# Joining the band stage to the recurrence: barrier taken out, gates made in the band, two z tiles moved, decay sums in rounded halves

## The reference, cut to what matters

```python
xn = _rmsnorm(h, norm_mix_w[l])
proj = xn @ w_in[l]
q_a, k_a, v_a, qkv_g, z_g, a_g, b_g = jnp.split(proj, SPLIT_POINTS, axis=-1)
attn = _windowed_gqa(q_a, k_a, v_a, band_bias, in_window, attn_sink[l])     # 8 heads, +-128 keys

# the mixer beside it
qkv = jax.nn.silu(_centred_conv(qkv, conv_w)).astype(f32)                   # 5 taps
q, k, v = jnp.split(qkv, 3, axis=-1)                                        # q, k then l2-normed
g = -jnp.exp(a_log.astype(f32)) * jax.nn.softplus(a + dt_bias.astype(f32))
beta = jax.nn.sigmoid(b)
o_fwd = _chunk_gated_delta_rule(q, k, v, g[:, :, 0], beta[:, :, 0])
o_bwd = flip(_chunk_gated_delta_rule(flip(q), flip(k), flip(v), flip(g[:, :, 1]), flip(beta[:, :, 1])))
o = _rmsnorm(o_fwd + o_bwd, norm_w) * jax.nn.silu(z)
h = h + jnp.concatenate([attn, gdn], axis=-1) @ w_out[l]
```

## Time and profile before

| | |
|---|---|
| median of 3 runs | 2480.06 us (2477.2 to 2482.18) |
| the profiled execution | 2485.23 us |
| its span in the trace | 2483.5 us |
| PE busy in it | 2390.8 us |
| band stage with a PE that is never idle | 108.4 to 372.9 us |
| from there to the first product of `front(0)` | 372.9 to 401.26 us |
| to `levels(0)` | 454.48 us |

### The profile page before, as it was taken

How to read it: one execution, slowest core, us unless ns; L and a number is a source line. 1 busy time by engine, 2 the same in 40 slices (tenths; PEclk the granted TensorE clock), 3 DMA queues, 4 the chain that set the end, 5 groups by cost and what they waited for, 6 DMA issues and landing times.

```text
span 2483.5 us, 32754 instructions
## 1 busy us (share of the span) xinstructions
PE 2390.8 (96%) x12918; PEld 2032.2 (82%) x12918; DVE 1071.9 (43%) x1652; ACT 803.6 (32%) x1353; POOL 750.2 (30%) x527
## 2 busy tenths in 40 slices
PE   7999996899899999999999999999999999999999
PEld 5888885899877888887888878988888788888887
DVE  5266624455445644352222253123333253556633
ACT  4144555222412422232121321144444112565101
POOL 2222112343322577762222223221111241111250
PEclk9999998899998999999999989999999999999999
DMA  6722212223343234344232205523441346343441
GB/s 207 224 58 62 68 53 70 63 57 75 118 144 112 86 118 170 119 138 159 93 99 71 68 17 210 156 75 86 113 119 51 132 161 158 106 109 140 135 160 68
DMA packets 252091, 274.95 MB, mean 111 GB/s; under 512 B 43730, under 2 KB 204280, under 8 KB 249897
## 3 DMA queue, kind: packets, MB, share of 16 engines
q1 hardware_dynamic: 229928, 217.31, 29.4%
q10 hardware_dynamic: 22016, 55.61, 6.1%
HBM read 188.91 MB, written 86.08 MB: 111 GB/s over the span
## 4 chain that ended last, share of the span: by engine, by line
PE 91%; DVE 3%; DMA 2%; ACT 1%; issue 1%; POOL 1%; POOLq 0%; SPq 0%; ACTq 0%; DVEq 0%
PE PS L302 19%; PE PS L1948 13%; PE PS L283 10%; PE PS L1929 10%; PE PS L2256 4%; PE PS L3059 4%; PE PS L2915 3%; PE PS L2211 3%; PE PS L2469 2%; PE PS L410 2%; PE PS L1961 2%; PE PS L1334 2%; PE PS L1328 2%; PE PS L706 1%; PE PS L2458 1%; PE PS L2754 1%
## 5 line engine op out<-in xcount | busy, mean ns | idle before, releaser
L250 POOL CAST Wh<-Wraw 128x1024 fp32r<-128x1024 f32 x72 | 75.8, 1053 | 882.2 <-PE PS L302 575.7
L1948 PE MATMUL PS<-op_h,fw_h 128*128 128x512 f32 x512 | 200.3, 391 | 3.6 <-POOL fw_l L1843 3.6
L1948 PE MATMUL PS<-op_l,fw_h 128*128 128x512 f32 x512 | 200.1, 391 | 0.0
L1948 PE MATMUL PS<-op_h,fw_l 128*128 128x512 f32 x512 | 200.1, 391 | 0.0
L252 POOL TENSOR_TENSOR Wl<-Wraw,Wh 128x1024 fp32r<-128x1024 f32 x72 | 176.3, 2448 | 10.4
L1843 POOL TENSOR_TENSOR fw_l<-draw,fw_h 128x512 fp32r<-128x512 f32 x64 | 84.7, 1325 | 257.8 <-ACT fw_h L1984 257.8
L1843 POOL TENSOR_TENSOR fw_l<-fraw,fw_h 128x512 fp32r<-128x512 f32 x92 | 126.3, 1386 | 95.5 <-ACT fw_h L1984 95.4
L1929 PE MATMUL PS<-op_h,fw_h 128*128 128x512 f32 x392 | 152.5, 389 | 0.0
L1929 PE MATMUL PS<-op_l,fw_h 128*128 128x512 f32 x392 | 152.5, 389 | 0.0
L1929 PE MATMUL PS<-op_h,fw_l 128*128 128x512 f32 x392 | 152.5, 389 | 0.0
L302 PE MATMUL PS<-XAh,Wh 128*128 128x512 f32 x328 | 134.3, 410 | 2.1 <-POOL Wl L252 2.1
(11 more groups left out here) (472 smaller groups left out, 5929.3 us busy)
## 6 DMA issues: line engine op xcount, KB each, us to landing
Wraw<-in_w_in SPq DMA_DIRECT2D x66, 512.0 KB, 4.2
fraw<-in_w_ffn_in SPq DMA_DIRECT2D x16, 1024.0 KB, 5.3
f_scr<-blocks SPq DMA_DIRECT2D x16, 1024.0 KB, 4.3
draw<-in_w_ffn_out SPq DMA_DIRECT2D x32, 512.0 KB, 4.1
stage<-f_scr SPq DMA_DIRECT2D x24, 512.0 KB, 4.6
x_scr<-hT SPq DMA_DIRECT2D x2, 4096.0 KB, 13.5
Wraw<-in_w_out SPq DMA_DIRECT2D x16, 512.0 KB, 4.0
gate_scr<-gbuf ACTq DMA_DIRECT2D x16, 512.0 KB, 2.7
```

The source lines that it names most:

```text
L250: pool.tensor_copy(Wh[:, slot], Wraw[:, slot])
L1948: mm = pe.matmul(dense_bank(n)[:, 512 * b:512 * b + 512], w_, x_, start=(k == 0 and m == 0), stop=(k == KT - 1 and m == 2))
```

## The change

Four things are done at once.

1. "phase1" joins `JOINED`: no barrier between band and recurrence. Buffers and PSUM banks are placed anew and waits are added in its stead.
2. The tile with a and b becomes the first of the tiles in the band. Its 8 transposes stand in unit 6, `act_softplus` and `dve_gates` in units 7 to 9, `pe_gates` behind the last unit. The zeros for `wy_scr` and `wt_scr` are written at the start of phase 1, from a buffer of zeros. The transposes of the recurrence's first chunk come ahead of the attention's last `turn_out`.
3. The band keeps 15 of the 17 tiles. The last two of z (96 products) are made in `pe_prep`: 8 products behind each of six chunks' transposes, the remaining 48 in a row ahead of `front(1)`. ACT takes them out and makes their silu behind `decays(1)`.
4. `gate` is divided into `gate_h` and `gate_l` (fp32r). `decay_rhs` makes two operands for each unit, and PE makes each decay sum as two fp32r products in place of one f32 product. ACT writes the exponentials into `qkT` in place of a buffer of their own.

Besides, `WY` and `WT` are loaded in eight pieces (the pieces for e = 0 first), the load for p = 0 waits until the last late product is made, and `load_att(sp, 0)` waits for the last update of the state (`d_s`, 7) where it waited for `d_o2` and `d_acc` of an earlier step.

```diff
-        BAND_FILL = list(range(N_CONV, N_AB + 1))
+        TILES = list(range(N_AB, N_OUT1))
+        LATE_Z = 2
+        BAND_FILL = TILES[:-LATE_Z]
+        AB_TURN = 6
...
             sp.dma_start(x_scr, hT[:]).then_inc(spill, 16)
+            sp.wait_ge(zeros_made, 1)
+            for scr in (wy_scr, wt_scr):
+                sp.dma_start(bass.AP(scr.tensor, 0, [[4 * GH * MAT // P, P], [4 * (P + 1), 4], [1, 4 * (P + 1)]]),
+                             zeros[:].unsqueeze(1).to_broadcast([P, 4, 4 * (P + 1)])).then_inc(setup_dma, 16)
...
             values(UW - 1)
-            pe.wait_ge(ab_sb, 1)
-            pe.wait_ge(w_pt, UW)
-            for t in range(NT):
-                mm = pe.transpose(PS[:, 4, t * 16:(t + 1) * 16], cpad[0][0:16, 2 + t * P:2 + (t + 1) * P], ident[0:16, 0:16])
-            mm.then_inc(ab_t, 1)
+            pe_gates(pe)
+            pe_turn_chunk(pe, 0)
             turn_out(NT - 1)
...
+            act_gates(act)
+            act_squares(act, 0)
             copy_out(NT - 1)
+            act_root(act, 0)
             store_out(NT - 1)
-            for i in range(2):
-                act.wait_ge(z_out[i], 32)
-            act.wait_ge(att_out, 32 * NT)
...
+        def late_z(pe):
+
+            for h in range(2 * LATE_Z):
+                f, b = Z0F + h // 2, h % 2
+                n = N_AB + f
+                if h == 0:
+                    pe.wait_ge(w_out, NT)
+                    pe.wait_ge(w_hi, NT)
+                elif b:
+                    pe.wait_ge(half_free, f + 1)
+                elif h == 2:
+                    pe.wait_ge(ps_free, n)
+                if b == 0:
+                    pe.wait_ge(w_ready, n + 1)
+                for c, (k, hi, lo) in enumerate(model):
+                    for w, x, m in ((Wh, hi, 0), (Wh, lo, 1), (Wl, hi, 2)):
+                        mm = pe.matmul(PS[:, Z_BANKS[h], :], w[:, n % 2, k], x[:, b * 512:(b + 1) * 512],
+                                       start=(c == 0 and m == 0), stop=(c == KT - 1 and m == 2))
...
-                if p >= 2:
+                if p == 0:
+                    sp.wait_ge(mm_done, N_OUT1)
+                elif p >= 2:
...
+                for e in range(2):
+                    for x, scr in ((WY_all, wy_scr), (WT_all, wt_scr)):
+                        for d in range(2):
+                            u = 2 * d + e
+                            sp.dma_start(x[p % 2][:, u], scr[u * GH:(u + 1) * GH, 0:P, :].rearrange("m p c -> p m c")
+                                         ).then_inc(wu_in[e], 16)
...
             for d in range(2):
-                sp.wait_ge(d_o2[d], NT - 2)
-                sp.wait_ge(d_acc[d], NT - 2)
+                sp.wait_ge(d_s[d], NT - 1)
+                sp.wait_ge(d_kd[d], NT)
+            sp.wait_ge(att_out, 32 * NT)
             load_att(sp, 0)
...
-                    pe.matmul(bank(d, 2 + e), tri[:, 2 + d], gl[e][d].rearrange("p h c -> p (h c)"), start=True, stop=True
-                              ).then_inc(d_dt[d], 1)
+                    for x in (gl_h[p // 2], gl_l[p // 2]):
+                        mm = pe.matmul(bank(d, 2 + e), strict[d][:], x[e][d].rearrange("p h c -> p (h c)"),
+                                       start=(x is gl_h[p // 2]), stop=(x is gl_l[p // 2]))
+                    mm.then_inc(d_dt[d], 1)
...
-            pe_prep(pe, 0)
+            fill = late_z(pe)
+            pe_prep(pe, 0, fill, (0, 8, 8, 8, 0))
             front(0)
             for d in range(2):
                 pe.wait_ge(d_kq[d], 2)
-            pe_prep(pe, 4)
+            pe_prep(pe, 4, fill, (8, 8, 8, 0, 0))
+            for _ in fill:
+                pass
             front(1)
...
+                if p == 0:
+                    pe.wait_ge(zeros_made, 2)
                 steps(p)
...
-        JOINED = ("phase5", "phase7", "phase9", "phase12", "phase14")
+        JOINED = ("phase1", "phase5", "phase7", "phase9", "phase12", "phase14")
```

More of the change, by code:

```diff
@@ L1015, in pe_prep @@
+        def pe_prep(pe, first, fill, quota):
+            for i in range(first, first + 5):
+                if i < first + 4 and i:
+                    pe_turn_chunk(pe, i)
+                for _ in range(quota[i - first]):
+                    next(fill)
                 if i > first:
@@ L1028, in act_softplus @@
             act.activation(gt[:, 1], gt[:, 0], ACT.Abs)
[L1029 removed]
+            act.activation(small[:, 0, 8:16], rows[:, 0:8], ACT.Exp)
             act.activation(beta[:], abT[:, :, 8:16], ACT.Exp, scale=-1.0).then_inc(beta_exp, 1)
@@ L1209, in sp_phase4 @@
                 sp.wait_ge(d_kd[d], NT)
+            for i in range(2):
+                sp.wait_ge(z_out[i], 32)
             sp.dma_start(zT[:], z_scr.rearrange("j p t -> p j t")).then_inc(z_back, 16)
@@ L1259, in pool_phase4 @@
             pool.wait_ge(blk_solved, 1)
+            qk_masked(0)
+            for d in range(2):
+                pool.wait_ge(d_dt[d], 4)
             k_gated(0)
-            qk_masked(0)
+            pool.wait_ge(mm_done, N_OUT1)
             k_decayed(0)
@@ L1265, in pool_phase4 @@
                     qk_masked(p + 1)
+                if p == 0:
+                    for i in range(LATE_Z):
+                        pool.wait_ge(z_out[i], 32)
+                    for d in range(2):
+                        pool.memset(St[d][:], 0.0)
+                    pool.memset(oacc[:], 0.0).then_inc(zeros_made, 1)
                 if p + 2 < NP2:
```

273 lines of the change are left out of this document (170 added, 103 removed).

## The result

The changed kernel takes 2464.8 us (median of 5, 2460.71 to 2469.49) where the kernel before takes 2480.06: a ratio of 0.9931, 95% interval 0.992 to 0.9943. It is faster by 15.3 us at the medians, 17 by the ratio. The forecast was 35 us with a range of 2435 to 2462, so the time lies outside it, on the slow side.

The account below looks back on a forecast made before the run. PE, busy 96% of the span, was taken as the bound. Terms -20.2 - 9.1 - 8.3 - 2.2 + 3.4 + 1 = -35.4 us; from the 2480.06 median this gave 2445 us, 8-in-10 range 2435 to 2462.

Parts of the forecast that it names:

- The band: Band before the recurrence: 96 products leave, saving 21.9 us; a and b add 0.7, hiccups 1; sum -20.2 us.
- the start: Kernel's start: 2 MB of zeros go ahead of `load_q(2)`, costing 0 to 5 us; +1 taken.
- B: Time mark from which the forecast counts: the end of the band's last values, 372.90 us in the trace before.
- the rival that the band is not PE's: In the band PE waits for DVE's maxima: total 2457, or 2467 if all 21.9 us are lost; chance 0.14.
- To `front(0)`: From the band's end to `front(0)`: starts at B+22 instead of B+28.4, 6.4 us less, with 24 moved products inside.
- `front(0)`: Recurrence's first front: 11.0 us at full clock, where it took 14.72 at clock 0.82; ends at B+33.0.
- Solving and the 48 products: After `front(0)`: blocks solved at B+57.0 without gain; 48 products (11.0) and a bank exchange (0.5) end at B+62.3.
- `levels(0)` at B+72.5: Start of the first pair's levels, where loads and `front(1)` meet: 9.1 us earlier than B+81.6.
- The first level at 8.85 us: First level of `levels(0)`: with PE hardly pausing before it, 8.85 us instead of 17.16, so -8.3 us.
- `front(2)` and `front(3)`: Later fronts of the recurrence: each saves 1.1 us, together -2.2.
- The end of the recurrence: Attention, `zT` and w_out loads queue behind the last state update; ACT's second rounding ends later: +3.4 us.
- The rival of the low clock: PE's clock stays low in the recurrence's first stretch: 8.3 us and up to 5 more, total 2458; chance 0.16.

Follow-up runs that it names:

- e8: Changed kernel, but DVE takes the attention's low part out of its bank between the first chunk's sum of squares and its root; ratio to the kernel before 0.9909.
- e6: Changed kernel, but ACT's two waits for stores stand ahead of the first late z half's eviction, not ahead of the exponentials; ratio to the kernel before 0.992.
- e9: Changed kernel, but 8 and 16 late z products fill the second preparation's last two slots, ACT emptying their bank one chunk earlier; `levels(0)` 9.7 us earlier, no total given.
- e1: Changed kernel, but solving of the next pair's blocks is not called in the first pair's first level; ratio to the kernel before 0.9907.
- e5: Changed kernel, but at the recurrence's end SP loads the w_out tiles first, then the attention's half, then zT; ratio to the kernel before 0.9911.
- e3: Kernel before the change, with the second pair's block solving not called in the first level, as in e1; ratio 0.9998.
- e4: Changed kernel without 92 of the 96 moved z products, every wait kept; ratio to the kernel before 0.992.
- e10: Changed kernel with the edits of e1, e5, e6, e8, e9, and POOL's `decay_rhs(2)` held until after the third level; 2438.4 us, ratio to the kernel before 0.9836.

## Why the prediction missed, step by step

Against the profiled execution of before, the forecast's sum was -35.4 us and the change gave -20.4.

- *The band: -20.2 was forecast, with +1 for the start.* B moved by 20.8. **Right**, and the rival that the band is not PE's falls: PE was busy for 262.6 of its 264.5 us, at clock 1.00.
- *To `front(0)`: B+22.* B+23.0, 5.4 us earlier than before where 6.4 was forecast. The late products began at B+7.8 (forecast 8.1), the low clock was foreseen. **Right**, though e8 shows that the order could be had at B+18.0.
- *`front(0)`: 11.0 us at full clock.* It took 14.1. **This step failed.** 1.3 us are the table load, for which the sum has no term; before the change it lay ahead of the wait and cost nothing (e6). Another 1.5 are clock, 0.88: at clock 1.00 it took 12.6 with the load still in it (e8), so 11.3 without, 0.3 above the sum. What the stage is made of was right, "at full clock" was not.
- *Solving and the 48 products: the last z product at B+62.3.* B+70.7, 8.4 us late. 4.1 us are inherited. From the end of `front(0)` to the row of 48 PE took 19.1 us where the sum had 17.8: 1.3. And the row took 14.5 us, partly at half clock, where the sum had 11.0 and 0.5 for a bank: 3.0. **This step failed** by the clock. The sum's 17.8 us left PE idle for part of the preparation, and gave what that does to the products behind it no price. The trace shows the pause, 3.4 us for the last chunk's k, and products 0.43 us apart behind it. With the slots filled (e9) the last product ends at B+61.0.
- *`levels(0)` at B+72.5: 9.1 us won.* B+80.1, 1.5 won. It follows from the two steps above. What stands between the last product and the level was about right: 10.2 us were forecast, 9.4 came. (The terms, 62.3 + 9.07 + 0.8, give 72.2; and the solved blocks' 57.0 and 4 give 61.0, not 61.4.) But `front(1)` alone bound it; PE didn't wait for the loads.
- *The first level at 8.85 us: -8.3.* 17.0 us, and 0.8 more in the second. **This is the largest failure**, 9.0 us. The step asked only what the clock would be. Next behind the clock was DVE's wait for `blkG`, of 6.73 us, with PE idle for 6.3 of the level. The trace of before had the row: a wait of 0.63 us for `blkG` in the middle of a level at half speed. A wait of 0.63 us in a level that is to be halved is a wait of several. 3.4 of the 6.1 us that it grew by could be read there; 1.6 came because `levels(0)` now follows `front(1)` at once, so that the store starts late. e1 shows what the wait cost: without it the level takes 8.85 us. The step also called POOL's zeroing of `oacc` covered, and asked only when PE would need it; DVE's copy beside it was held, about 1 us of the 6.3.
- *`front(2)` and `front(3)`: -1.1 each.* From the start of `front(2)` to `levels(1)` 9.55 us against 10.67, -1.12, and 9.54 against 10.68 in `front(3)`. **Right.**
- *The end of the recurrence: +3.4.* +5.4. The mechanism was right, the term was too small by 2.0. Counted from the start of the last state update's products, ACT was to end its second rounding at 17.6 us, with only that one, of 1.04 us, left when the second tile landed. ACT's rounding began at 17.5 us, and both tiles were rounded in a row, 2.00 us: the second tile didn't come later than the first's rounding. e5 gives it all back.
- *Later.* The sum had nothing there; the spans of the two profiled executions differ by another 2.5 us. In the feed-forward stage PE waits once for POOL's part of a weight, in both kernels; here is the product behind that wait and the one after the next, before and now:

```profile
1131.67 0.77 PE L1948 MATMUL PS<-op_h,fw_h 128*128 128x512 f32 x1 [3.60 <-POOL fw_l L1843]
...
1132.66 0.63 PE L1948 MATMUL PS<-op_h,fw_l 128*128 128x512 f32 x1
```

```profile
1110.44 0.47 PE L2082 MATMUL PS<-op_h,fw_h 128*128 128x512 f32 x1 [2.08 <-POOL fw_l L1977]
...
1110.97 0.40 PE L2082 MATMUL PS<-op_h,fw_l 128*128 128x512 f32 x1
```

Before, some 12 products behind the wait stand 0.43 us apart, now 0.23. It isn't only these two executions. In both kernels without the change (before and e3) the wait is 3.60 and 2.83 us and the products behind it run at half clock; in all eleven with it the wait is 1.87 to 2.63 us and they run at full clock. So the change seems to shorten a wait 700 us later. By what path, no run shows.

Sum of the misses to the mark where DVE goes on: +7.6 to `levels(0)`, +9.0 in its levels, +2.0 at the end, and -1.6 for the band with the start; 17.0 of the 35.4, and 18.3 us were won there.

The rival of the low clock had half of it. Clocks of 0.76 between 400 and 414 us and 0.75 in the first level are what it named. A pause of 3.4 to 3.6 us, at `late_z` and in the last slot, is followed by products at 0.43 us, and without it (e8, e9) the clock is 1.00. The rule of the Trainium skill named there (TensorE: Matmul & The Clock Gate, "A second HAM failure mode: psum-queue depth-cycling") speaks of frequent short idling between groups of products. These are single pauses of 3.4 to 3.6 us, so the trace agrees that idling brings the low clock and doesn't show the rule's own case. But the rival priced a level at half speed. What the first level cost was a wait, and with the wait gone the clock there was 1.00 (e1). So a rival at 2458 was nearer, with the wrong mechanism for its largest term.

That the late products themselves cost the kernel anything like the 21.9 us that they saved in the band is not what e4 shows: without them `levels(0)` comes 7.6 us earlier, and the time falls by some 3. But e4 lost part of its gain in a slow first level, and they were not taken out of a kernel without that wait. e10 keeps them, with its other edits, and begins `levels(0)` 5.7 us earlier than e4. The change was sound; the places around it were not ready for it.

What stays open: when a level behind an idle PE runs at half speed and when not (0.91 in one execution, 0.52 in another, the same code there), why DVE is sometimes let in between POOL's operations and sometimes not until the last, and how the change reaches the wait in the feed-forward stage.

## What to carry to other kernels

When a change makes a stage faster, look for waits in that stage which are short only because it is slow: on an engine that takes its work in order, a wait of half a microsecond for a round trip is a deadline, and everything queued behind it inherits the miss. Ask also what used to start that round trip early. A pause of PE here cost itself and about as much again in clock: 2.3 us less of one was worth 5.0 at the next mark (e8). And a product moved into an idle slot needs its bank, its weights and its reader there too, or it trades one wait for another.

## What the runs showed of the hardware

- A small DVE operation with both inputs in SBUF, 0.18 us alone, took 0.83 and 0.94 us beside POOL's operations of 1.04 us, which read SBUF, and once 7.81: it waits for the end of one of them, or of the whole row. With one input in PSUM it isn't slowed (0.42). Beside a memset an operation with two SBUF inputs isn't either, but a copy from SBUF to SBUF is (1.45 and 1.21 for 0.18), and PSUM operations behind that copy end with it (1.36 us for 0.41).
- Where the waits of an activation stand decides when its table is loaded. Behind two more waits the load of 1.28 us began only when the last of the operands was there (381.06); with these two waits moved ahead it was made at 375.16, 6 us before its use (e6).
- Products of 128x512 follow one another at 0.43 us behind a pause of PE of 3.56 us (359.90), of 3.41 us and another 0.69 (408.29), and of 3.60 and 2.83 us in the feed-forward stage of the two kernels without the change; behind pauses of 1.87 to 2.63 us in the same place, and of 1.22 us in e8, at 0.23.
